# Products whose moving columns are streamed, and written, from the last to the first

## The reference

```
p = h @ w_in[l]
x = x + g1 * gated_merge(p[..., QKV_END:], y_conv, y_attn, w_out[l])
u = dwconv1d(h @ w_up, dw, dw_b)
return (jax.nn.silu(g) * a) @ w_down
...
proj = u @ w_in[l]
h = h + jnp.concatenate([a_out, b_out, c_out], axis=-1) @ w_out[l]
h = h + jnp.square(jax.nn.relu(u @ w_ff1[l])) @ w_ff2[l]
```

## Time and profile before

| | |
|---|---|
| median of 3 runs | 1969.24 us (1968.95 to 1971.2) |
| the profiled execution, its own time | 1968.53 us |
| its span, first to last instruction | 1966.7 us |
| TensorE busy with matmuls | 1907.7 us, 97% |
| weight loads (beside the matmuls) | 1645.9 us, 84% |
| VectorE, ScalarE, GpSimd busy | 54%, 45%, 60% |
| mean granted TensorE clock | 0.994 of full speed |
| DMA | 306.57 MB, mean 156 GB/s |

### The profile page before, as it was taken

One profiled execution on the slowest core, in us unless ns is written; L12 is line 12 of the kernel. 1 busy time (PEld: TensorE's weight loads), 2 busy tenths in 40 slices (PEclk: granted clock), 3 DMA queues, 4 the chain that ended last, 5 costly groups with the idle time before them and its releaser, 6 DMA issues.

```text
span 1966.7 us, 34019 instructions
## 1 busy us (share of the span) xinstructions
PE 1907.7 (97%) x12494; PEld 1645.9 (84%) x12494; DVE 1062.1 (54%) x1988; ACT 889.5 (45%) x1517; POOL 1185.6 (60%) x904
## 2 busy tenths in 40 slices
PE   7999999999999999999999999999999999999997
PEld 4687777888888887877889999787899998779997
DVE  4899865354443324887647743875542038554402
ACT  3223444243433323525546645556554354555533
POOL 2444233424654554635569987673788876649895
PEclk9999999999999999999999999999999999999999
DMA  9942233628433343436455575532465564326563
GB/s 387 358 125 79 55 96 116 229 78 174 138 111 106 118 150 124 147 89 217 142 194 182 181 238 162 163 108 88 132 182 180 172 201 141 110 76 197 188 190 111
DMA packets 121976, 306.57 MB, mean 156 GB/s; under 512 B 29688, under 2 KB 52600, under 8 KB 121476
## 3 DMA queue, kind: packets, MB, share of 16 engines
q1 hardware_dynamic: 119096, 300.16, 47.4%
q10 hardware_dynamic: 2764, 4.80, 1.5%
HBM read 300.19 MB, written 8.06 MB: 157 GB/s over the span
## 4 chain that ended last, share of the span: by engine, by line
issue 36%; POOL 30%; PE 29%; DVE 4%; ACT 1%; POOLq 0%; ACTq 0%; DVEq 0%
POOL w_lo L781 30%; PE bank L1325 9%; PE bank L1326 8%; PE bank L1327 8%; DVE nb L2152 1%; PE bank L1897 1%; PE bank L1899 1%; PE bank L1898 1%; DVE v_lo L2152 1%; DVE rinv L2144 0%; ACT w_hi L824 0%; PE bank L2078 0%; DVE u_lo L2144 0%; POOLq L775 0%; DVE rho L2157 0%
## 5 line engine op out<-in xcount | busy, mean ns | idle before, releaser
L781 POOL TENSOR_TENSOR w_lo<-raw,w_hi 128x512 fp32r<-128x512 f32 x884 | 1167.6, 1347 | 762.6 <-ACT w_hi L824 760.5
L824 ACT ACTIVATE w_hi<-raw 128x1024 fp32r<-128x1024 f32 x442 | 465.9, 1056 | 291.6 <-PE bank L1327 211.6
L1325 PE MATMUL bank<-h_hi,w_hi 128*128 128x256 f32 (+1 forms) x1248 | 426.9, 342 | 4.6 <-POOL w_lo L781 2.7
L1326 PE MATMUL bank<-h_lo,w_hi 128*128 128x256 f32 (+1 forms) x1248 | 418.3, 335 | 0.0
L1327 PE MATMUL bank<-h_hi,w_lo 128*128 128x256 f32 (+1 forms) x1248 | 418.2, 335 | 0.0
L1325 PEld LDWEIGHTS bank<-h_hi,w_hi 128*128 128x128 f32 x1248 | 237.0, 190 | 46.5 <-issue 13.3
L1327 PEld LDWEIGHTS bank<-h_hi,w_lo 128*128 128x128 f32 x1248 | 236.9, 190 | 24.7
L1326 PEld LDWEIGHTS bank<-h_lo,w_hi 128*128 128x128 f32 x1248 | 237.2, 190 | 23.3 <-issue 0.2
L1325 PE MATMUL bank<-u_hi,w_hi 128*128 128x272 f32 (+1 forms) x736 | 211.7, 288 | 0.3 <-DVE u_lo L2152 0.3
L1326 PE MATMUL bank<-u_lo,w_hi 128*128 128x272 f32 (+1 forms) x736 | 210.0, 285 | 0.0
L1327 PE MATMUL bank<-u_hi,w_lo 128*128 128x272 f32 (+1 forms) x736 | 209.1, 284 | 0.0
(11 more groups left out here) (381 smaller groups left out, 3641.1 us busy)
## 6 DMA issues: line engine op xcount, KB each, us to landing
raw<-in_wstream SPq DMA_DIRECT2D x442, 512.0 KB, 3.5
ada_raw<-in_wada SPq DMA_DIRECT2D x48, 512.0 KB, 13.3
late_a<-in_wada SPq DMA_DIRECT2D x16, 512.0 KB, 5.4
late_b<-in_wada SPq DMA_DIRECT2D x16, 512.0 KB, 4.5
biash<-rpb_by_offset SPq DMA_DIRECT2D x64, 64.0 KB, 2.6
gates<-in_wada SPq DMA_DIRECT2D x8, 512.0 KB, 4.9
rpb_by_offset<-in_rpb SPq DMA_DIRECT2D x16, 224.0 KB
bias_by_distance<-vec ACTq DMA_DIRECT2D x1, 3264.0 KB
```

What stands on the lines that cost most here:

```text
L781: i = pool.tensor_tensor(lo[:, part, s, :], whole[:, part, :], hi[:, part, s, :].bitcast(F32), ALU.subtract)
L824: act.activation(w_hi[q >= first["l2", 0]][:, :, s, :], raw[:, s, :].rearrange("p (g c) -> p g c", c=PAIR), ACT.Copy)\
L1325: pe.matmul(o, hi, a_hi, start=start, stop=False)
L1326: pe.matmul(o, hi, a_lo, start=False, stop=False)
```

## The change

The helper turns the three views around before it issues its matmuls: the output, and the high and low parts of the activation, are walked from the last column to the first, with a step of -1. The stationary operand, the order of the instructions, the waits, the addresses of all tiles and everything that does not go through `three` stay as they are. Column c of the activation still gives column c of the output, since both are turned.

```diff
@@ -1322,6 +1322,7 @@
                 n = i >= first["l2", 0]
                 g, h = (k % 4, k // 4) if n else (k // 2, k % 2)
                 hi, lo = (w[n][:, g, i % RING, h * P:(h + 1) * P] for w in (w_hi, w_lo))
+                o, a_hi, a_lo = (x[:, ::-1] for x in (o, a_hi, a_lo))
                 pe.matmul(o, hi, a_hi, start=start, stop=False)
                 pe.matmul(o, hi, a_lo, start=False, stop=False)
                 return pe.matmul(o, lo, a_hi, start=False, stop=stop)
```

## The result

The changed kernel takes 1985.51 us (median of 4 runs, 1983.7 to 1986.58) against 1969.29 us before. The ratio is 1.0076, with a 95% interval of 1.0064 to 1.0087. I had forecast 1957 us. The profiled execution took 1986.58 us, with a span of 1984.8 us where before it was 1966.7.

The account below looks back on a forecast made before the run. TensorE's product rate was taken as the bound, with some 12.4 ns excess on each of 10128 products. Moving read 12 us less, all else nothing: 1968.5 - 12 = 1956.5, so 1957 us; range 1908 to 2030, leaving out half rate.

Parts of the forecast that it names:

- The moving read: Operand reads in `three`: turning changes how often moving and weight reads meet; 4848 matmuls gain 2.5 ns each, 12 us less.
- the excess: Time per product beyond its columns' own, in `three`: 12.4 ns on each of 10128 products, about 125 us.
- the value of the nearest rows with another place: Products at 13.3 ns: 116.9 and 115.6 against 120 ns, less what a mixture leaves, taken as 2.5 ns gain each.
- the dearest bound of everything: Products moving columns out of weight areas, 233 ns, 6.3 above 226.7; at 10128 x 6 ns, 61 us more.
- For the other 5280 I take nothing: The remaining matmuls of `three`, already at mixed places: no gain or loss counted.
- The write into PSUM: Output bank written downwards: taken at nothing, since the same words of the same bank are written once.
- the rival of half the column rate: All products: neighbouring columns joined only in upward order; 1407 us more, 3375 us; chance 0.12.
- What reads behind it: Bank readers and GpSimd after each product: order hidden; GpSimd's 104 ns a product cuts nothing from the gain.
- The reads meet more often: Every product of `three`: turned reads meet the weights' read more, up to 6 ns each, 61 us, 2030 us; chance 0.22.
- Direction does not matter: All products: excess could be a weight-changing cost, equal in both directions; 1969 us; chance 0.26.
- the excess still the same for both widths: Sign in start distances, above 226.7 and 120.0 ns, that the reads meet more often.
- growing with the columns: Sign in start distances of half the column rate: near 427 and 214 ns.

Follow-up runs that it names:

- the sweeps: TensorE alone, no part of the reference computed: groups of 12 products, varying operand places and read direction; 512 columns upwards at offset 0 226.7 ns, downwards 233.4.

## Why the prediction was wrong

*The step that failed* is "The moving read". Its first half, that the excess hangs on where the two operands lie relative to each other, was right for an upward read: the sweeps show 226.6 to 234.9 ns for one instruction by place alone. Its second half, that turning the read puts it at another such place, was not: a downward read of 512 columns stood at 233.2 to 233.4 ns at 15 offsets, so turning takes the good place away and gives no other. And the size had the wrong sign, because I did not see on which side of the range the kernel stands. I took "the value of the nearest rows with another place" from rows of 256 columns, where the layout of `h` is a poor place, and gave it to 2736 products of 512 columns, for which it is the best place there is. The row for them with another place was in my hands: 233 ns. I had used it as the dearest bound of everything. Taken as the 512-column value it gives 2736 x (233 - 226.7) = +17 us. The term stood in the sum as 2736 x 2.5 ns = 7 us less; measured, these products lost 6.0 ns each, 15.7 us over the pairs. That rows 9 and a downward read both stand at 233 ns is an agreement of numbers, and no run shows a common cause. The 13.3 ns that both widths share looked like one quantity and was two: the lowest excess of one width and nearly the highest of the other.

*Narrow products.* Of the terms, 2112 products with 256 columns at 13.3 ns were to gain 2.5 ns each. They gained 1.5 ns each, 3.0 us. "For the other 5280 I take nothing" was near: gains and losses of 1 to 6 ns mostly cancel, and what is left is a loss of 2.8 us (3.5 with 256 columns, -0.6 with 272). That all the narrow products together cost nothing is this coincidence.

*The write into PSUM*, taken at nothing: right, ratio 1.0000 with the write turned alone. The page "PSUM — Partial Sum Buffer" of the Trainium skill, Specifications (TRN2), says that any non-contiguous pattern slows matmuls significantly. A step of -1, and blocks of 16 bytes turned in themselves, are not slowed at all here. With them the rival of half the column rate is gone: no product in fp32r came near 427 ns.

*What reads behind it.* In sum no wait came or went in the changed kernel, as said. But that nothing would be cut from a gain down to 112 ns a product was wrong. With `h` at 115.7 ns in the mean, 5.3 of 7.5 us came back as waits, 2.9 us of them at eight slabs whose second piece ended late. A mean of 104 ns a product did not say what a single slab waits for.

*The rivals.* "The reads meet more often" had the right sign, and its dearest row was the right row. Its picture was not: the excess was to spread over all 10128 products and both widths, and it fell on 2736. What "reads meet" should mean is open besides: the width of the weights changes an upward read's distance and does nothing to a downward read of 512 columns. "Direction does not matter" holds for the narrow products in sum and for the write. The two signs that I had named for a slower kernel ("the excess still the same for both widths" or "growing with the columns") do not describe it: 512 columns lost and 256 columns out of `h` gained. One slip of the sum changed nothing: 125 us over 10128 products is 12.3 ns each, not 12.4.

*What stays open.* Why a downward read of 512 columns loses its good place, what 16-byte blocks have to do with it, and why earlier groups leave a trace in later ones. The order in which the weights are read was not varied.

## What to carry over

A rate that looks like a constant across shapes may be the best case of one shape and the worst of another, so compare each shape only with rows of its own width, above all before giving a change the sign of a gain. When an effect depends on the place of operands, a group of a dozen products on the engine alone, over a few offsets, shows within one run where a layout stands between its best and worst. And before paying work for a faster product, see what comes back as waits: of 7.5 us saved by place in one layer 5.3 were returned.

## What was unexpected of the hardware

The distance of products in fp32r isn't a constant on top of the columns. Many settings stand on steps of 6.67 ns, 16 columns' time at 2.4 GHz: 113.3 and 120.0 for 256 columns, 226.7 and 233.3 for 512. The page "TensorE: Matmul & The Clock Gate" of the Trainium skill, Back-to-back issue gap, puts some 2.5 ns there. No group in fp32r here with 256 columns or more came below some 6.5 ns (113.2 - 106.7). In plain float32 the figure does return: the records stood 215.8 ns apart with 256 columns and 429.1 with 512, which is 2.5 ns above twice 106.7 and twice 213.3. Reversing columns inside 64-byte blocks adds a quarter to the columns' time (266.7 against 213.3 ns), which is far more than reversing the whole run (233.3), while reversing them inside 16-byte blocks costs nothing. And from 128 to 240 columns such a product costs some 111.6 ns, however many columns of these it has.
